# Input rows and meta tokens given by columns, with the row factor applied behind the first products

## The chip, the cores and the metric

The kernel runs on one core of one Trainium2 chip. Its five engines run side by side and wait for one another through semaphores: TensorE (PE in the profile, its weight loads PEld), VectorE (DVE), ScalarE (ACT), GpSimd (POOL) and SyncE (SP), which here only issues transfers. The metric is the device time of one execution in microseconds; lower is better. The kernel before takes 978.37 us, the median of three runs that lie between 978.27 and 979.35 us.

## The reference

Two transformer blocks are computed one after the other on 256 rows of width 1024. Only the start of the first block matters here. Sixteen meta tokens are put before the 256 input rows (272 rows together), and each row is normalised and projected:

```python
u = rms_norm(h, pre_mix_gain[l])          # each row times rsqrt(mean(row^2) + 1e-6), each column times a gain
proj = u @ w_in[l]
qa, ka, va, qb, kb, vb, g = jnp.split(proj, SPLITS, axis=-1)
qa = rope(qa...); ka = rope(ka...); qb = rope(qb...); kb = rope(kb...)
o_swa = windowed_gqa_sink_attention(qa, ka, va, attn_sink[l], pos, is_real)
o_diff = differential_attention(qb, kb, vb, lam, lambda_init, diff_subln_gain[l], is_key)
gates = jax.nn.sigmoid(g + b_gate[l])
```

`rope` multiplies by cosines and sines of the position and adds the two halves of a head; the rest of the block (two attentions, gates, output projection, feed-forward) and the whole second block follow. All of it is float32. The norm is a factor of the row times a gain of the column. A factor of the row can be applied before the product with `w_in` or behind it.

## The kernel before

**Products.** A float32 product is made of three products in a reduced format. Each weight tile is split on ACT into a rounded part `whi` (line 1968) and on DVE into the rest `wlo = raw - whi` (line 1338); the activations are split the same way into `R1[0]` and `R1[1]`. PE then adds whi x R1[0], whi x R1[1] and wlo x R1[0] (lines 796 to 798, and 920 to 922 for the first unit).

**Units and halves.** Weights come in units of 1 MB (1024 x 256 columns, 128x8x256 in a tile), four buffers `raw` deep, issued by SP at line 2515; buffer i is used again once the unit four before is split (the wait at line 2514). A unit is worked in two halves, 24 products each. A function, `schedule()`, writes one list of steps, and each engine runs in this order the steps that it knows. "ahead" steps put the splits up to four halves ahead of PE, as far as the two buffers `whi`, `wlo` allow. An engine works its own list strictly in order, so a wait holds everything behind it on that engine.

**The opening.** SP loads the input rows X, ACT issues meta tokens, the identity and the gains. ACT and DVE square the 272 rows, POOL takes the power -0.5 (line 2356), ACT and DVE scale the rows (`rows`), PE turns them to columns (`turn` and `turnm`, line 782), and ACT and DVE split them with the gain into R1 (lines 2002 and 1389). While nothing is there, PE multiplies a constant 13 times (`keep`, line 787).

**The first units.** They are: unit 0 (two blocks of `qa`), unit 1 (`ka0`), unit 2 (`va`), unit 3 (more `qa`). For each block of a query or key, ACT copies the PSUM bank with halves swapped in four pieces (line 2019, `rope` or `roped`), DVE multiplies by the cosine and sine tables (lines 1421 and 1422), POOL adds (line 2368). `swap` copies the two key blocks with their halves exchanged into KS (lines 2027 and 2028). The values go through `VT` (line 2034), a turn on PE and a copy on DVE (lines 1428 to 1435). `setup` makes small constants of the parameters; its exponential on ACT (line 2011) waits for two dot products on DVE.

**The first head.** The scores of the first head (line 941) stand on PE after the first half of unit 3. They need all of `qa` block 0, both key blocks (`rope_pool ("ka0", 1)`) and both copies of `swap` (`swap_act`). What stands behind them on PE waits too, the second half of unit 3 first. `gate(u)` is the gate's product with a tanh straight from PSUM (line 2093).

## Time and profile before

| | |
|---|---|
| median of three runs | 978.37 us |
| the profiled execution, its own time | 978.03 us |
| its span, first to last instruction | 976.2 us |
| PE busy | 949.0 us (97%) |
| DVE busy | 685.8 us (70%) |
| ACT busy | 533.3 us (55%) |
| mean granted TensorE clock | 0.995 |

The profiled execution is 0.34 us under the median, and 1.8 us of it lie outside the span. A row of the timeline gives start, duration, engine, line, operation, output<-inputs, count, and in brackets the idle time ahead of it and what ended it. Line 1962 is the helper through which all of ACT's work goes, 1338 the low split of weights, 1331 a scalar multiply on DVE. A granted clock of 1.00 is 2.4 GHz, 0.50 is 1.2 GHz. PE's matmuls overlap, so their durations do not add up; what counts is the distance from start to start.

### The profile page before, as it was taken

The page shows a single profiled execution, that of the slowest core. Times are in us where ns is not written, and L with a number is a line of the kernel's source. Part 1 is how long each engine was busy: PE and PEld are TensorE (multiplying, and loading weights), DVE is VectorE, ACT ScalarE, POOL GpSimd, SP SyncE. Part 2 cuts the span into 40 slices and gives each one's busy share as a digit, 9 for nine tenths or more (in the row PEclk, how much of TensorE's full clock was granted, in tenths as well). Part 3 has the DMA queues.
Part 4 walks back from the last instruction along what each step waited for, and adds up shares of the span by engine and source line. Part 5 has one row for each costly group of instructions (what it writes and reads, how often), then busy time and mean ns, then how long its engine had stood idle before and what let it go on. Part 6 is the DMA issues. An engine that isn't in the chain of part 4 may idle for free.

```text
span 976.2 us, 15556 instructions
## 1 busy us (share of the span) xinstructions
PE 949.0 (97%) x6212; PEld 846.6 (87%) x6212; DVE 685.8 (70%) x1251; ACT 533.3 (55%) x1019; POOL 126.4 (13%) x145
## 2 busy tenths in 40 slices
PE   8999999999999999999999999799899999999997
PEld 7999888999999988888988898698699898888885
DVE  6888776777478676766667679776665577676765
ACT  7876666765456643434355877444444364434443
POOL 2211111211032000000001139610100000000001
PEclk9999999999999999999999999999999999999999
DMA  9543334334377556565647642201353446656541
GB/s 319 188 135 131 130 112 148 99 120 134 126 260 236 174 174 215 173 216 173 204 141 247 224 165 88 87 1 44 131 172 130 151 132 210 199 170 200 171 169 43
DMA packets 115863, 154.71 MB, mean 158 GB/s; under 512 B 2728, under 2 KB 98224, under 8 KB 115536
## 3 DMA queue, kind: packets, MB, share of 16 engines
q1 hardware_dynamic: 113376, 142.91, 44.4%
q0 software_dynamic: 1952, 10.42, 3.0%
q8 instruction: 49, 0.80, 0.4%
q10 hardware_dynamic: 464, 0.40, 0.2%
q14 instruction: 22, 0.18, 0.1%
HBM read 150.56 MB, written 3.16 MB: 157 GB/s over the span
## 4 chain that ended last, share of the span: by engine, by line
PE 84%; DVE 8%; ACT 5%; issue 2%; DMA 0%; POOL 0%; POOLq 0%; DVEq 0%; ACTq 0%
PE ps L820 14%; PE ps L796 8%; PE ps L798 8%; PE ps L797 8%; PE ps L821 7%; PE ps L1107 4%; PE ps L1080 4%; PE ps L1081 4%; PE ps L1082 4%; PE ps L839 3%; PE ps L841 3%; PE ps L840 3%; PE ps L782 3%; DVE wlo L1338 2%; PE ps L809 2%; PE ps L811 2%
## 5 line engine op out<-in xcount | busy, mean ns | idle before, releaser
L1338 DVE TENSOR_TENSOR wlo<-raw,whi 128x1024 fp32r<-128x1024 f32 (+1 forms) x268 | 326.8, 1237 | 161.2 <-ACT whi L1962 160.9
L1962 ACT ACTIVATE whi<-raw 128x1024 fp32r<-128x1024 f32 (+1 forms) x268 | 274.2, 1051 | 132.8 <-PE ps L821 53.8
L820 PE MATMUL ps<-R1b,whi 128*128 128x512 f32 x576 | 201.8, 393 | 0.0
L796 PE MATMUL ps<-R1b,whi 128*128 128x256 f32 (+1 forms) x592 | 172.6, 291 | 0.8 <-DVE wlo L1338 0.8
L798 PE MATMUL ps<-R1b,wlo 128*128 128x256 f32 (+1 forms) x592 | 167.7, 283 | 0.0
L797 PE MATMUL ps<-R1b,whi 128*128 128x256 f32 (+1 forms) x592 | 167.6, 283 | 0.0
L821 PE MATMUL ps<-R1b,wlo 128*128 128x256 f32 x576 | 161.4, 280 | 0.0
L820 PEld LDWEIGHTS ps<-R1b,whi 128*128 128x128 f32 x576 | 108.1, 188 | 24.7 <-issue 0.5
L796 PEld LDWEIGHTS ps<-R1b,whi 128*128 128x128 f32 x592 | 111.5, 188 | 10.1 <-issue 7.9
L798 PEld LDWEIGHTS ps<-R1b,wlo 128*128 128x128 f32 x592 | 111.8, 189 | 0.0
L797 PEld LDWEIGHTS ps<-R1b,whi 128*128 128x128 f32 x592 | 111.5, 188 | 0.2
L821 PEld LDWEIGHTS ps<-R1b,wlo 128*128 128x128 f32 x576 | 108.2, 188 | 0.6
L2356 POOL TENSOR_TENSOR st<-st 128x1 f32<-128x1 f32 (+5 forms) x28 | 23.1, 832 | 382.4 <-DVE st L1331 299.8
L1080 PE MATMUL ps<-whi,R3ah 128*128 128x512 f32 x176 | 69.0, 392 | 1.1 <-DVE wlo L1338 1.1
L1081 PE MATMUL ps<-wlo,R3ah 128*128 128x512 f32 x176 | 68.8, 391 | 0.0
L1082 PE MATMUL ps<-whi,R3al 128*128 128x512 f32 x176 | 68.5, 389 | 0.0
L1962 ACT ACTIVATE F<-F 128x512 f32<-128x512 f32 (+6 forms) x58 | 29.3, 506 | 55.3 <-DVE F L1591 53.7
L1962 ACT ACTIVATE R3ah<-F 128x512 fp32r<-128x512 f32 x22 | 13.9, 632 | 67.8 <-DVE F L1613 67.8
L1580 DVE TENSOR_REDUCE F<-ps 128x256 f32<-128x512 f32 x72 | 49.3, 685 | 0.0
L1962 ACT ACTIVATE SC<-ps 128x512 f32<-128x512 f32 (+3 forms) x78 | 33.1, 429 | 22.8 <-PE ps L798 10.4
L1080 PEld LDWEIGHTS ps<-whi,R3ah 128*128 128x128 f32 x176 | 33.0, 188 | 9.1 <-issue 1.9
L1082 PEld LDWEIGHTS ps<-whi,R3al 128*128 128x128 f32 x176 | 33.0, 188 | 7.2
(294 smaller groups left out, 1801.3 us busy)
## 6 DMA issues: line engine op xcount, KB each, us to landing
raw<-in_w_in SPq DMA_DIRECT2D x34, 1024.0 KB, 5.0
raw<-in_w_ffn_in SPq DMA_DIRECT2D x22, 1024.0 KB, 5.1
raw<-in_w_ffn_out SPq DMA_DIRECT2D x11, 1024.0 KB, 5.5
raw<-in_w_gate SPq DMA_DIRECT2D x11, 1024.0 KB, 5.4
raw<-in_w_up SPq DMA_DIRECT2D x11, 1024.0 KB, 5.3
raw<-in_w_down SPq DMA_DIRECT2D x11, 1024.0 KB, 5.6
raw<-in_w_out SPq DMA_DIRECT2D x8, 1024.0 KB, 5.1
raw<-in_w_xkv SPq DMA_DIRECT2D x8, 1024.0 KB, 5.4
```

What stands on the lines that cost most here:

```text
L796: e.matmul(o, hi[:, kt, c], R[0][:, kt, 0:n], start=kt == 0, stop=False)
L797: e.matmul(o, hi[:, kt, c], R[1][:, kt, 0:n], start=False, stop=False)
L798: m = e.matmul(o, lo[:, kt, c], R[0][:, kt, 0:n], start=False, stop=kt == 7)
L820: e.matmul(B[:, :].rearrange("p (a n) -> p a n", a=2), hi[:, kt, c], R[2][:, :, kt, 0:256], start=kt == 0, stop=False)
L821: m = e.matmul(B[:, 0:256], lo[:, kt, c], R[0][:, kt, 0:256], start=False, stop=kt == 7)
L1080: e.matmul(B[:, :], Fh[:, k, c], hi[:, k, d], start=j == 0 and k == 0, stop=False)
L1081: e.matmul(B[:, :], Fh[:, k, c], lo[:, k, d], start=False, stop=False)
L1082: m = e.matmul(B[:, :], Fl[:, k, c], hi[:, k, d], start=False, stop=end and k == 1)
L1107: return e.matmul(o, a, b, start=True, stop=True)
L1338: e.tensor_tensor(half_of(wlo[i % HL], i, k), half_of(raw[i % RAW], i, k), f32(half_of(whi[i % HL], i, k)), SUB).then_inc(lo_split(i, (i, k)))
L1580: e.tensor_reduce(FSLOT[j % 2][0][:, at:at + 256], B[:, :].rearrange("p (a n) -> p n a", a=2), AX, ADD).then_inc(ffn_dve((kind, f, j, b)))
L1962: return e.activation(o, i, f, **kw)
```

## The change

The host now also gives the input rows and the meta tokens by columns (`x_cols`: 8 gains and 8 x 272 columns on 128 partitions, 1092 KB). They come in two halves, the first unit of weights in two halves too. R1 is split straight from them (`xsplit`), without the row factor, so that the norm's statistics and the turns on PE are no longer ahead of the first products. The row factor is applied behind the products: PE spreads it over the partitions (`rowtab`), DVE multiplies it into the cosine and sine tables and keeps a copy for the gates; values get it in the copy behind their turn; a gate's product is multiplied by it on DVE, and tanh reads that (`tanh`). The rows as such, for the statistics and for the residual, come behind unit 2, all on SP. The first unit's products go pass by pass (`ropek`). The first four blocks of `rope` take their PSUM bank from the pool "head". `swap` stands one half later, behind `setup`, `rowtab` and four rope blocks.

```diff
     def opening():
+        def laid(k, key, b):
+            step("roped", key, b, k)
+            step("rotate", key, b, k)
         order.append(("w_in", "featk", 0, 256))
         for j in range(2):
             take(0, j)
             step("ropek", j, 0)
...
+        order.append(("w_in", "feat", 1024, 256))
+        for j in range(2):
+            take(1, j)
+            step("ropep", "ka0", j, j, 1, 2 + j)
+            if j == 0:
+                step("rowstat")
+            yield 1
+        state["rope"] = 4
+        for j, _ in enumerate(values("va", 1280, 0, ("setup",))):
+            if j == 0:
+                step("rowtab")
+                laid(0, "qa", 0)
+                laid(1, "qa", 1)
+            else:
+                laid(2, "ka0", 0)
+                laid(3, "ka0", 1)
+                step("swap")
+            yield 1
...
     def gates(u):
-        return unit(("gate", u), "w_in", "feat", 4608 + 256 * u)
+        yield from unit(("gate", u), "w_in", "feat", 4608 + 256 * u)
+        step("tanh", u)
...
-    step("rows", "n1")
+    step("xsplit", 0, 4)
     ahead(1)
-    step("turn", "n1", (0, 2))
-    ahead(2)
-    step("turn", "n1", (4, 6))
-    step("turnm")
+    step("xsplit", 4, 8)
...
+            def rowtab():                                   # PE
+                B = claim("head", ("row0",), (norm_dve, "tables"))
+                p.wait_ge(id_in, 0)
+                p.wait_ge(norm_pool, "row0")
+                for i in range(2):
+                    mm(B[:, 128 * i:128 * i + 128], rs0[:, i:i + 1].to_broadcast([128, 128]), ident)
...
-                B = claim("gemm", ("rope", k), (rope_act, k), (rope_dve, ("cos", k)))
+                B = claim("head" if k < 4 else "gemm", ("rope", k), (rope_act, k), (rope_dve, ("cos", k)))
...
+                p.wait_ge(hi_split, (i, part))
+                for w, r in ((hi, 0), (hi, 1), (lo, 0)):
+                    if w is lo:
+                        p.wait_ge(lo_split, (i, part))
...
+            def xsplit(first, end):                         # DVE
+                for kt in range(first, end):
+                    d.wait_ge(norm_act, ("n1", "hi", kt))
+                    stt(R1[1][:, kt, :], xT[:, kt, :], xcols[:, kt:kt + 1], f32(R1[0][:, kt, :]), MUL, SUB)...
+            def rowtab():                                   # DVE
+                B = ps("row0")
+                d.wait_ge(norm_pe, "row0")
+                d.wait_ge(ca_in, 0)
+                for name in ("cos", "sin"):
+                    e.tensor_tensor(caf(name), caf(name), B[:, 0:NT], MUL).then_inc(norm_dve("tables"))
+                d.wait_ge(set_act, "lam")
+                e.tensor_copy(rsb0, B[:, 0:256]).then_inc(norm_dve("tables"))
...
+            def gate(u, j, i):                              # DVE
+                if j:
+                    d.wait_ge(gemm, ("gate", u))
+                    d.wait_ge(norm_dve, "tables")
+                    e.tensor_tensor(GA[:, 2 * u:2 * u + 2, :], ps("gate", u)..., rep(rsb0, 2), MUL).then_inc(gate_dve(u))
...
+            def xsplit(first, end):                         # ACT
+                a.wait_ge(xb_in if first else xa_in, 0)
+                for kt in range(first, end):
+                    act(R1[0][:, kt, :], xT[:, kt, :], scale=xcols[:, kt:kt + 1]).then_inc(norm_act(("n1", "hi", kt)))
+            def rowstat():                                  # ACT
+                for signal_, v_, m, i in ((x_in, X[:, 0, :], 128, 0), (meta_in, metat, 16, 2)):
+                    a.wait_ge(signal_, 0)
+                    act(sq0[i][0:m], v_, ACT.Square, accum_out=row0[0:m, i:i + 1]).then_inc(norm_act("sq0"))
```

On SP, which issues nearly all transfers, this is the order before, from the first one on:

```order
L2509 DMA X<-in_x 128x1024
L2510 DMA X<-in_x 128x1024
L2515 DMA raw<-in_w_in 128x8x256
L2517 DMA ca<-in_const_a 128x544
L2515 DMA raw<-in_w_in 128x8x256
L2519 DMA pc<-in_params 128x391
L2520 DMA ca<-in_const_a 128x544
```

and now (`F<-in_x_cols` are the columns, the two `128x4x256` the halves of unit 0, `ca` 128x128 the identity, the first `ca` 128x544 the cosine and sine tables, the second the masks):

```order
L2563 DMA F<-in_x_cols 128x1096
L2568 DMA raw<-in_w_in 128x4x256
L2569 DMA F<-in_x_cols 128x1088
L2570 DMA raw<-in_w_in 128x4x256
L2574 DMA raw<-in_w_in 128x8x256 x2
L2576 DMA X<-in_x 128x1024
L2577 DMA X<-in_x 128x1024
L2578 DMA F<-in_meta_tokens 16x1024
L2579 DMA ca<-in_const_a 128x128
L2580 DMA ca<-in_const_a 128x544
L2581 DMA pc<-in_params 128x399
```

Behind both lists come the further units: before, units 2 and 3 with nothing between them; now unit 3, the masks and unit 4. The rows X have moved from the front to behind unit 2, and what ACT issued is now on SP ahead of unit 3.

On ACT, from the split of units 1 and 2 to the exponential of `setup` (`whi` is a split, SE, SC and SD with 32 partitions are rope copies, SD 128x272 is a value block, F<-F 64x272 is `swap`, st<-st 128x2 the exponential), before:

```order
L1962 ACTIVATE whi<-raw 128x8x128 x3
L1962 ACTIVATE SE<-ps 32x256 x4
L1962 ACTIVATE SC<-ps 32x256 x4
L1962 ACTIVATE whi<-raw 128x8x128
L1962 ACTIVATE SD<-ps 32x272 x4
L1962 ACTIVATE whi<-raw 128x8x128
L1962 ACTIVATE SE<-ps 32x272 x4
L1962 ACTIVATE whi<-raw 128x8x128
L1962 ACTIVATE SD<-ps 128x272
L1962 ACTIVATE F<-F 64x272 x4
L1962 ACTIVATE st<-st 128x2
```

and now, from the squares of the rows (`F,st<-`) to `swap`:

```order
L2009 ACTIVATE F,st<-X 128x1024
L2009 ACTIVATE F,st<-F 16x1024
L2009 ACTIVATE whi<-raw 128x8x128 x2
L2009 ACTIVATE SD<-ps 128x272
L2009 ACTIVATE st<-st 128x2
L2009 ACTIVATE SE<-ps 32x256 x4
L2009 ACTIVATE SC<-ps 32x256 x4
L2009 ACTIVATE whi<-raw 128x8x128
L2009 ACTIVATE SD<-ps 128x272
L2009 ACTIVATE SD<-ps 32x272 x4
L2009 ACTIVATE SE<-ps 32x272 x4
L2009 ACTIVATE F<-F 64x272 x4
```

The two splits ahead of the value block are now those of unit 3, the exponential stands ahead of all four rope blocks, and these are worked in one go between unit 3's splits and `swap`. PE's own list is the same from the first scores to the end (5180 rows in either); ahead of them it has 18 rows fewer.

## Rows read from the trace of the kernel before

**Rows 1.** The page: the span, and PE's busy time.

```profile
span 976.2 us, 15556 instructions
PE 949.0 (97%) x6212; PEld 846.6 (87%) x6212; DVE 685.8 (70%) x1251; ACT 533.3 (55%) x1019; POOL 126.4 (13%) x145
```

**Rows 2.** Windows: length; PE, PEld, DVE, ACT, POOL busy (count); clock; DMA share; GB/s.

```profile
3.75:22.50 18.75, 16.31 (x118) 14.84 (x117) 13.58 (x26) 14.01 (x27) 2.79 (x4) 1.00 1.09 357
60.00:80.00 20.00, 20.00 (x165) 18.17 (x165) 16.64 (x48) 15.45 (x38) 2.88 (x4) 1.00 0.49 158
...
618.70:621.20 2.50, 2.50 (x11) 2.50 (x12) 2.50 (x4) 0.39 (x1) 2.39 (x3) 0.50 0.00 0
```

**Rows 3.** Waits of PE from 30 to 260 us: total, times, longest.

```profile
PE ps L941 <- ACT SC L1962: 2.0, 4, 0.6
```

**Rows 4.** Timeline of PE, opening to the first scores.

```profile
0.93 7.34 PE L787 MATMUL ps<-st 128*128 128x256 f32 x26 [0.93 <-DVE st L1950]
...
12.69 0.36 PE L920 MATMUL ps<-R1b,whi 128*128 128x256 f32 x1 [0.85 <-DVE R1b L1328]
...
19.31 0.36 PE L796 MATMUL ps<-R1b,whi 128*128 128x272 f32 x1 [0.77 <-DVE wlo L1338]
...
34.67 0.49 PE L782 MATMUL ps<-ca,SD 128*128 128x128 f32 x3
35.09 1.56 PE L941 MATMUL ps<-F 64*128 64x272 f32 x8
```

**Rows 5.** Timeline of SP: the issue of unit 3.

```profile
7.87 2.92 SPq L2515 DMA_DIRECT2D raw<-in_w_in  x1
```

**Rows 6.** Time from issue to landing: the first half of X, then unit 3.

```profile
X<-in_x SPq DMA_DIRECT2D x1, 512.0 KB, 4.2
...
DMA to landing us min/median/max: 12.6/12.6/12.6
```

**Rows 7.** Timeline of ACT, the first square to the exponential of `setup`.

```profile
4.91 1.06 ACT L1962 ACTIVATE F<-X 128x1024 f32<-128x1024 f32 x1 [1.50 <-DMA X<-in_x]
...
17.81 1.99 ACT L1962 ACTIVATE whi<-raw 128x1024 fp32r<-128x1024 f32 x2
19.83 1.58 ACT L1962 ACTIVATE SE<-ps 32x256 f32<-32x256 f32 x4
...
26.86 1.63 ACT L1962 ACTIVATE SE<-ps 32x272 f32<-32x272 f32 x4
28.51 1.06 ACT L1962 ACTIVATE whi<-raw 128x1024 fp32r<-128x1024 f32 x1
29.60 0.40 ACT L1962 ACTIVATE SD<-ps 128x272 f32<-128x272 f32 x1
30.20 1.79 ACT L1962 ACTIVATE F<-F 64x272 f32<-64x272 f32 x4 [0.20 <-POOL F L2368]
32.01 0.20 ACT L1962 ACTIVATE st<-st 128x2 f32<-128x2 f32 x1
```

**Rows 8.** Timeline of DVE: low splits, a sine product, the start of `setup`, a 512 copy.

```profile
17.94 3.50 DVE L1338 TENSOR_TENSOR wlo<-raw,whi 128x1024 fp32r<-128x1024 f32 x3 [0.66 <-ACT whi L1962]
...
28.88 0.43 DVE L1422 TENSOR_TENSOR SE<-SE,ca 128x272 f32<-128x272 f32 x1
...
31.17 0.16 DVE L1331 TENSOR_SCALAR st<-pc 128x16 f32<-128x16 f32 x1
...
51.95 0.68 DVE L1468 COPY SC<-ps 128x512 f32<-128x512 f32 x1
```

**Rows 9.** Timeline of POOL: the three powers, and the sum of the second key block.

```profile
6.39 2.63 POOL L2356 TENSOR_TENSOR st<-st 128x1 f32<-128x1 f32 x3 [4.58 <-DVE st L1331]
...
29.39 0.77 POOL L2368 TENSOR_TENSOR F<-SE 128x272 f32<-128x272 f32 x1 [1.97 <-DVE SE L1422]
```

**Rows 10.** Timeline of PE late in the program, where it had stood idle.

```profile
618.70 3.45 PE L1107 MATMUL ps<-SC 128*128 128x128 f32 x16 [2.62 <-DVE SC L1718]
...
634.03 2.59 PE L1107 MATMUL ps<-SC 128*128 128x128 f32 x16 [2.31 <-DVE SC L1718]
```

More of the change, by code:

```diff
@@ L340, in opening, with values @@
             step("ropek", j, 0)
-            if j:
-                for b in range(2):
-                    step("roped", "qa", b, b)
-                    step("rotate", "qa", b, b)
-                state["rope"] = 2
-            yield 1
-    def values(key, col0, u):
+            yield 1
+        order.append(("w_in", "feat", 1024, 256))
[16 more added lines that the diff above has]
+            yield 1
+    def values(key, col0, u, *then):
         order.append(("w_in", "feat", col0 + 256 * u, 256))
@@ L356, in values @@
                 step("vt", key, u, 0)
+            else:
+                for s in then:
+                    step(*s)
             yield 1
@@ L383, in schedule @@
     kb = [behind(kb[u], ("vt", "vb", u, 1)) for u in range(4)]
-    va = behind(values("va", 1280, 0), ("swap",), ("setup",))
-    units = [opening(), rope("ka0", 1024, 0), va, qa[1], ga[0], qa[2], ga[1], qa[3], ga[2], qb[0], vb[0], kb[0],
+    units = [opening(), qa[1], ga[0], qa[2], ga[1], qa[3], ga[2], qb[0], vb[0], kb[0],
              ga[3], qb[1], vb[1], kb[1], ga[4], qb[2], vb[2], kb[2], ga[5], qb[3], vb[3], kb[3], ga[6], *bs, ga[7]]
@@ L391, in schedule @@
                   [[]] * 5 + [[("merge", u)] for u in range(3)])
-    n = len(units) * 2
+    n = 2 * len(units) + 4
     at += [(n - 6, 1, ("between",))]
@@ L2085, in diff, with tanh @@
                     act(R3b[0][:, h, :], ps("O", x)[:, 256:512], scale=subg).then_inc(head_act(("oh", x)))
-            def gate(u, j, i):
-                if j:
-                    a.wait_ge(pc_in, 0)
-                    a.wait_ge(gemm, ("gate", u))
-                    a.wait_ge(set_dve, "hb")
-                    for k in range(2):
-                        act(GA[:, 2 * u + k, :], ps("gate", u)[:, 256 * k:256 * k + 256], ACT.Tanh,
-                            bias=hb[:, 2 * u + k:2 * u + k + 1], scale=0.5).then_inc(gate_act(u))
+            def tanh(u):
+                a.wait_ge(gate_dve, u)
+                a.wait_ge(set_dve, "hb")
+                for k in range(2):
+                    act(GA[:, 2 * u + k, :], GA[:, 2 * u + k, :], ACT.Tanh, bias=hb[:, 2 * u + k:2 * u + k + 1],
+                        scale=0.5).then_inc(gate_act(u))
             def merge(u):
```

134 lines of the change are left out of this document (72 added, 62 removed).

## The prediction

> **What bounds the kernel now.** I read the page first: PE is busy for 949.0 of 976.2 us [rows 1], so only what moves PE's work in time, or makes it wait, can count. Windows come next. From 60 to 80 us PE is busy for all 20.00 us with 165 products, 0.121 us from one to the next, while DVE has 16.64 and ACT 15.45 us of work [rows 2]; the waits say the same: from 30 to 260 us PE waits for another engine 4 times, 2.0 us in all, each time for exponentials ahead of scores [rows 3]. The reader is to see that behind the opening PE runs at its own rate, and that what is lost or won ahead of that stretch arrives at the end unchanged. Then PE's timeline: constant products until 8.27, first real product at 12.69, the second unit at 19.31, and from there without a gap to the first scores at 35.09 [rows 4]. So the start costs time, and the change goes for it. PE's list is the same from the first scores to the end, so one number decides: when these scores start, 35.09 us now. The last view is therefore of what the scores need: transfers, ACT, DVE and POOL up to there [rows 5 to 9].
>
> **The opening (removed: statistics, scaling and turns ahead of the products).** The first half of the columns is about as large as the first half of X, which landed 4.2 us after its issue and was being read at 4.91 [rows 6, 7]. Four column splits at 0.40 (the 128x272 copy) and a weight split of 1.0 [rows 7] put the first product at some 7.6 us in place of 12.69, where the 12 constant products end too. The second unit is bound by its transfer. Measured, the queue is never slack: 357 GB/s from 3.75 to 22.50 us [rows 2]. Unit 3 landed at 7.87 + 12.6 = 20.5 us [rows 5, 6] as the last of 5992 KB (X 1024, meta 64, units 0 to 3 4096, identity 64, tables 272, parameters 200, masks 272). Now 6812 KB come up to it (columns 1092, X, meta, identity, tables, parameters 204, four units; the masks come behind). That is 820 KB or 0.84 MB more, 2.35 us at 357 GB/s: **unit 3 lands at 22.8 us**. Unit 1 lands 3672 KB before it, 10.5 us earlier, at 12.3; with a split of 1.0 and a low split of 3.50/3 = 1.17 [rows 7, 8] PE starts it at 14.5 in place of 19.31. That is the gain, 4.8 us, if it survives.
>
> **What is late next.** The scores wait for `swap`, `swap` for the second key block's sum, and now all four rope copies stand on ACT behind unit 3's two splits and behind the exponential. Nothing of this could start earlier. X and the meta tokens land 1560 KB ahead of unit 3, at 18.3, their second square (1.06 plus some 0.2 for its sum [rows 7]) ends at 19.6, and ACT then stands before unit 3's split with nothing else to do, 3.2 us. The steps, each at its measured length:
> - 22.8, two splits, 1.99 [rows 7]: 24.9 with the start's delay of 0.1. The second low split on DVE behind them, 1.17 after the first, which ends at 25.1 [rows 8]: 26.3.
> - `setup` starts behind these low splits; from its first instruction at 31.17 to the exponential at 32.01 it took 0.84 [rows 7, 8]. Exponential at 27.1, ACT free of it by 27.2.
> - Two rope copies of 1.60 each with their gap: 30.4. A split of unit 4, 1.08: 31.5. The value copy, 0.42: 31.9. Two key copies of 1.65 each: 35.2 [rows 7].
> - From the end of the last key copy (26.86 + 1.63 = 28.49) DVE's cosine and sine products, POOL's sum (29.39, 0.77) and `swap` took until 30.20 + 1.79 = 31.99, 3.50 us [rows 7 to 9]: **38.7**.
>
> The scores start at 38.7 in place of 35.09: **+3.6 us**, and the 4.8 us won are idle time of PE ahead of them. The row factor itself is in time: POOL's three powers took 2.63 [rows 9], one now covers all three columns, so it is ready by 21; DVE's tables follow the exponential at 28.3, ahead of the second rope copy's end. One smaller wait shows: PE's first value turn takes the bank that these tables free, about 28.3 against the 26.5 at which PE is there (five halves and a turn took 34.67 + 0.33 - 19.31 = 15.7, 3.0 us a half [rows 4]). It is covered by the larger one behind it. Bounds of this term: if unit 3 landed as early as before, the chain would start with the value block at 23.5 and end at 35.5, +0.4; with DVE and POOL getting in each other's way on every step as badly as the rows allow, one more us, +4.6. I take 3.6, since each item has its own row.
>
> **The clock.** PE is through with the first half of unit 3 and the second value turn at about 32.4, so it stands idle for 6.3 us ahead of the scores. Idle stretches of 2.62 and 2.31 us stand late in the program [rows 10], and behind the first one the granted clock is 0.50 for 2.5 us of work, which is 1.2 GHz, half the work at the same time: 1.25 us lost in that window [rows 2]. The new stretch is over twice as long and ahead of dense products. I take 1.5 us, between 0 (the early waits near 0.8 us [rows 4] cost nothing) and 2.5. The Trainium skill, "TensorE: Matmul & The Clock Gate", section on HAM oscillation, says that a wait between groups of matmuls sends the array back to its low clock and that the next group starts cold. This trace agrees (0.50 behind the 2.62 us of idle); by that rule the sum is the one below, without it 1.5 us less.
>
> **The other edits.** Eight gate products get a DVE multiply of 512 columns from PSUM, priced by the 512 copy at 0.68 us [rows 8]: 5.4 us more on DVE between 45 and 250 us. They lie beside PE's work, in DVE's free 3.36 of 20 us [rows 2], and tanh reads SBUF instead of PSUM at about the same length. If such a multiply falls ahead of a maximum that scores wait for, one of the four waits [rows 3] grows by up to 0.68: between 0 and 2.7 us. I take 0.3, since the four waits have only 2.0 us together and the multiply is off that chain in most places. The value copies become multiplies of the same size, the memset and the three small matmuls of `rowtab` (the turn of similar size took 0.49 [rows 4]) lie in time that PE waits anyway, and the first unit pass by pass has the same 48 products. The transfers moved from ACT to SP add no bytes and are counted above. Unit 4 lands 1296 KB (itself and the masks) behind unit 3, 3.7 us later at 26.5, long before PE asks for it.
>
> **Sum.** 3.6 + 1.5 + 0.3 = 5.4 us. The profiled execution's own time is 978.03 with a span of 976.2 and 1.8 us around it; 983.4 on its scale, 0.34 more on that of the median: **983.8 us**.
>
> **The rivals.**
> - *S, the late transfer is not late.* If the first transfers moved faster than the 357 GB/s of the rows, unit 3's split would be bound by PE (the first buffers come free with unit 1's second half at 20.5) and the chain by the value block at 23.5. The scores then start at 35.5, +0.4, and with the idle stretch of 4 us the clock may add 0 to 1.5: 978.8 to 980.5, taken as 979.6. For it: large rows of 4 KB in the columns. Against it: a share of 1.09 with all 16 engines busy already [rows 2]. The Trainium skill, "DMA: Bandwidth & Descriptors", section "Anatomy of one DMA", gives about 2.0 us plus bytes over 436 GB/s for a transfer issued on POOL; the 6.98 MB would then be in at 0.7 + 2.0 + 16.0 = 18.7 us, an estimate from that page. The trace does not agree, with 357 GB/s.
> - *C, the stall without the clock.* As forecast, but the clock stays at 1.00: 982.3. For it: 1.50 us and less of idle early on cost nothing. Against: both late stretches.
> - *G, the gates tip DVE.* DVE has 83% in the window of 60 to 80 us [rows 2]; if seven multiplies each delay a low split or a maximum that PE is about to need, 7 x 0.68 = 4.8 us come on top: 988.6. Against: low splits run up to four halves ahead.
> - *F, the opening's gain arrives.* If `swap` were through when PE comes to the scores, PE would start them at 14.5 + 5 x 3.0 + 2 turns of 0.5 = 30.5, 4.6 us ahead: 973.8. It decides for this if the exponential is over by 18.9 us, since ACT and its followers need 11.6 us from there. Against it stand unit 3's landing and its two splits in ACT's own list ahead of it.
>
> **How the numbers follow.** Forecast 62%, C 16%, S 10%, G 6%, F 4%, and 2% that the change does nothing that can be seen (978.4). A measurement of this kernel tells some 0.2%, 2.0 us, from no change. Slower by more: the forecast, C, G and a third of S, 0.87; within: two thirds of S and the rest, 0.09; faster: F, 0.04. The range takes in the forecast with a us off in the chain and the clock between its bounds, C and the upper part of S: 980.2 to 986.8.
>
> **What would show it.** In the profile after: first product near 7.6 and unit 1 near 14.5; ACT idle for about 3 us ahead of unit 3's first split, which starts near 22.9; exponential near 27.1; the first scores at 38.7 with an idle stretch ahead of them that ends with ACT's F<-F copies; a clock near 0.50 right there; PE busy all through 60 to 80 us. I am wrong if the scores start before 35 us, if unit 3's split starts before 21, or if PE has new waits behind 60 us of over 1 us in sum.

## The result, and the profile after

The changed kernel takes 988.74 us (median; 986.42 to 989.21), the kernel before beside it 978.32 us (978.05 to 979.35): a ratio of 1.0108, 95% interval [1.0095, 1.0121]. It is slower, as forecast, but by 10.4 us in place of 5.4, and outside the range of 980.2 to 986.8.

The page of the changed kernel (span, then busy time of each engine), to be held against [rows 1]:

```profile
span 984.6 us, 15518 instructions
PE 950.3 (97%) x6192; PEld 847.2 (86%) x6192; DVE 689.2 (70%) x1255; ACT 533.2 (54%) x1016; POOL 125.6 (13%) x143
```

PE has 1.3 us more busy time; the rest of the 8.4 us of span is idle. Of the four timed runs the profiled one is the fastest (986.42), so the span tells less than the median. A mark in the program tells more: the first product of 512 columns in the first feed-forward (FFN) starts at 339.7 us in place of 329.6, 10.1 us late, which agrees with the medians. These are the groups of that product, in the kernel before and in the changed one (shortest, median and longest in ns, then first and last start):

```profile
L820 PE MATMUL ps<-R1b,whi x576: 387/393/470, 329.6 to 940.5; 128*128 128x512 f32 x192
```

```profile
L843 PE MATMUL ps<-R1b,whi x576: 387/393/470, 339.7 to 948.9; 128*128 128x512 f32 x192
```

Behind the mark the two profiled executions differ by 1.7 us the other way (648.4 and 646.7 us of device time). Runs of one kernel fall into groups 1 to 2 us apart (the kernel before, beside later runs: 976.3 to 977.1 and 977.8 to 978.7 us), so a median can come from either, and a difference of less than 2 us is better read at the mark. All ledgers below stop at that mark.

The opening first. PE's timeline (start, duration, tile, shape, count, and what ended the idle time before), against [rows 4]:

```profile
8.88 2.25 PE L945 MATMUL ps<-R1b,whi 128*128 128x256 f32 x16
...
29.75 0.55 PE L805 MATMUL ps<-ca,SD 128*128 128x128 f32 x3 [1.73 <-DVE pc L1435]
...
40.66 2.19 PE L964 MATMUL ps<-F 64*128 64x272 f32 x8 [7.07 <-issue]
```

The first product starts 3.8 us sooner (8.88 against 12.69), and PE is at the first value turn (L805) at 28.0 us, where it waits until 29.75; in the kernel before the same turn starts at 31.50. All that is won there is idle time ahead of the scores at 40.66. The first product itself waited for no data: the first weights were split at 7.2 us (ACT 6.19 + 1.04), but PE multiplied constants until 8.9. What the scores waited for is on ACT (against [rows 7]):

```profile
18.09 1.06 ACT L2009 ACTIVATE F<-F 16x1024 f32<-16x1024 f32 x1
...
23.91 2.01 ACT L2009 ACTIVATE whi<-raw 128x1024 fp32r<-128x1024 f32 x2 [4.67 <-DMA raw<-in_w_in]
25.82 0.38 ACT L2009 ACTIVATE SD<-ps 128x272 f32<-128x272 f32 x1
28.02 0.21 ACT L2009 ACTIVATE st<-st 128x2 f32<-128x2 f32 x1 [1.82 <-DVE st L1357]
28.25 1.57 ACT L2009 ACTIVATE SE<-ps 32x256 f32<-32x256 f32 x4
...
34.60 1.62 ACT L2009 ACTIVATE SE<-ps 32x272 f32<-32x272 f32 x4
38.63 1.78 ACT L2009 ACTIVATE F<-F 64x272 f32<-64x272 f32 x4 [2.41 <-POOL F L2421]
```

It is the chain of the forecast, link by link, and each link later than forecast: unit 3's splits at 23.9 (22.9), exponential 28.0 (27.1), end of the last key copy 36.2 (35.2), end of `swap` 40.4 (38.7). From the splits to the last key copy it took 12.3 us, as forecast; only the landing and the last step are longer. The last step took 4.2 us in place of 3.5: DVE began it 0.3 us behind the key copy, being still at the block before, and then met POOL (against [rows 8, 9]):

```profile
36.90 0.87 DVE L1459 TENSOR_TENSOR SE<-SE,ca 128x272 f32<-128x272 f32 x1
```

```profile
36.71 0.76 POOL L2421 TENSOR_TENSOR F<-SD 128x272 f32<-128x272 f32 x1 [3.69 <-DVE SD L1459]
```

The sine product, begun 0.19 us behind POOL's sum, takes 0.87 us, against 0.43 without one; POOL's sum has its usual 0.76.

The windows (length; PE, PEld, DVE, ACT, POOL busy; clock; DMA share; GB/s), against [rows 2]:

```profile
0.75:24.00 23.25, 23.07 (x146) 21.60 (x147) 11.98 (x20) 12.98 (x20) 1.92 (x3) 1.00 1.02 339
...
42.00:44.00 2.00, 2.00 (x9) 1.30 (x8) 1.94 (x5) 1.93 (x4) 0.00 (x0) 0.50 0.12 27
...
60.00:80.00 20.00, 19.64 (x155) 16.92 (x154) 15.23 (x36) 14.89 (x36) 2.42 (x4) 1.00 0.45 148
```

Transfers ran at 339 GB/s on the mean of a window that holds their start; from 3.75 to 22.50 us, the stretch of [rows 2], it is 362 GB/s against 357, so they were no slower. Behind the 7.07 us of idle the clock is 0.50 (1.2 GHz); and between 60 and 80 us PE, which had not one idle stretch there before, has 0.36 us of it. That last line is the part of the loss that the forecast did not have. The waits of PE from 30 to 260 us (total, times, longest), against [rows 3]:

```profile
PE ps L964 <- issue: 7.1, 1, 7.1
PE ps L964 <- ACT SC L2009: 3.4, 4, 1.4
PE ps L805 <- DVE pc L1435: 1.7, 1, 1.7
PE ps L994 <- DVE SC L1509: 1.0, 2, 0.7
```

What PE waited 2.0 us for on ACT ahead of scores it now waits 3.4 us for, and a wait for DVE's copy ahead of the probabilities' turn (L994) is new. One of its two places, in DVE's rows and then in PE's; the gate's multiply (L1560) stands right ahead of the copies:

```profile
71.69 0.68 DVE L1560 TENSOR_TENSOR SE<-ps,pc 128x512 f32<-128x512 f32 x1
72.29 0.68 DVE L1507 COPY SC<-ps 128x512 f32<-128x512 f32 x1
72.89 0.28 DVE L1509 COPY SC<-ps 128x128 f32<-128x128 f32 x1
```

```profile
73.22 0.71 PE L994 MATMUL ps<-SC,SD 128*128 128x128 f32 x4 [0.36 <-DVE SC L1509]
```

So the ledger to the mark is: first scores +5.6 (35.09 to 40.66); from there to the second scores +1.25 (10.21 to 11.46, the clock); from there to the mark +3.3 (284.3 to 287.6), of which 2.4 us are these waits and the other 0.8 to 0.9 us do not show as idle.

### The profile page after: what moved, and what is told of

It is laid out like the page before. It is cut to its first block, busy times and chain, and to the rows that moved or that the text cites. A ratio compares the mean times of both kernels' runs of the same rounds, so it can differ in the third digit from the quotient of the medians.

```text
span 984.6 us, 15518 instructions
## 1 busy us (share of the span) xinstructions
PE 950.3 (97%) x6192; PEld 847.2 (86%) x6192; DVE 689.2 (70%) x1255; ACT 533.2 (54%) x1016; POOL 125.6 (13%) x143
## 4 chain that ended last, share of the span: by engine, by line
PE 76%; DVE 11%; ACT 8%; issue 2%; DMA 1%; SPq 1%; POOL 0%; POOLq 0%; DVEq 0%; ACTq 0%
PE ps L843 14%; PE ps L844 7%; PE ps L819 6%; PE ps L821 6%; PE ps L820 6%; PE ps L1130 4%; PE ps L1103 4%; PE ps L1104 4%; PE ps L1105 4%; PE ps L862 3%; PE ps L864 3%; PE ps L863 3%; DVE wlo L1361 3%; ACT whi L2009 3%; PE ps L805 2%
## 5 line engine op out<-in xcount | busy, mean ns | idle before, releaser
L843 PEld LDWEIGHTS ps<-R1b,whi 128*128 128x128 f32 x576 | 108.1, 188 | 24.7 <-issue 0.5
L2405 POOL TENSOR_TENSOR st<-st 128x2 f32<-128x2 f32 (+5 forms) x26 | 21.4, 825 | 396.7 <-DVE st L1354 313.9
```

The costliest lines, as they stand in the source:

```text
L843: e.matmul(B[:, :].rearrange("p (a n) -> p a n", a=2), hi[:, kt, c], R[2][:, :, kt, 0:256], start=kt == 0, stop=False)
```

## The experiments

The table gives for every kernel the start of the first and second scores, the mark, and the last distance, all of the profiled execution; then the median and the ratio to the kernel before as it ran beside that kernel (its medians there were 977.8 to 978.3 us). The diffs are cut: `...` stands for what is left out. In the rows with * the heads stand later in PE's list, so that more products precede the scores, and only the mark compares.

| kernel | first | second | mark | second to mark | median us | ratio [95%] |
|---|---|---|---|---|---|---|
| before | 35.09 | 45.30 | 329.6 | 284.3 | 978.32 | |
| after | 40.66 | 52.12 | 339.7 | 287.6 | 988.74 | 1.0108 [1.0095, 1.0121] |
| gates_alone | 35.05 | 45.28 | 333.8 | 288.5 | 980.71 | 1.0034 [1.0023, 1.0044] |
| gates_psum | 40.34 | 52.08 | 336.5 | 284.4 | 985.12 | 1.0077 [1.0050, 1.0103] |
| gates_behind | 40.48 | 52.94 | 344.0 | 291.1 | 991.30 | 1.0145 [1.0130, 1.0160] |
| gates_short | 40.95 | 53.68 | 338.7 | 285.0 | 987.06 | 1.0098 [1.0084, 1.0111] |
| gates_pool | 40.89 | 53.26 | 337.7 | 284.4 | 985.34 | 1.0079 [1.0067, 1.0091] |
| warm_gap | 41.30 | 51.14 | 339.7 | 288.6 | 987.60 | 1.0099 [1.0076, 1.0122] |
| copies_first | 38.42 | 49.67 | 337.5 | 287.8 | 986.62 | 1.0089 [1.0072, 1.0106] |
| copies_gates | 38.53 | 50.91 | 341.9 | 291.0 | 988.79 | 1.0120 [1.0105, 1.0135] |
| rotates_first | 37.42 | 49.92 | 337.3 | 287.4 | 985.29 | 1.0074 [1.0061, 1.0086] |
| best | 37.41 | 47.25 | 333.4 | 286.2 | 981.76 | 1.0041 [1.0027, 1.0056] |
| tables_first | 36.38 | 46.30 | 332.5 | 286.2 | 981.67 | 1.0036 [1.0023, 1.0049] |
| scores_later * | 40.23 | 52.37 | 337.4 | | 985.77 | 1.0080 [1.0055, 1.0104] |
| all_early_7 * | 42.54 | 52.37 | 339.4 | | 986.03 | 1.0092 [1.0077, 1.0107] |
| tables_first_7 * | 37.68 | 47.51 | 330.4 | | 978.95 | 1.0008 [0.9999, 1.0017] |
| one_ahead_7 * | 36.46 | 46.39 | 330.5 | | 979.04 | 1.0008 [0.9998, 1.0018] |
| one_ahead_7b * | 36.63 | 48.05 | 330.6 | | 977.64 | 1.0005 [0.9996, 1.0015] |

**gates_alone**: the kernel before, with nothing but the multiply on DVE (by a row of ones) and the hyperbolic tangent behind it, one step later.

```diff
+        step("tanh", u)
...
+                    e.tensor_tensor(GA[:, 2 * u:2 * u + 2, :], ps("gate", u)[:, :]..., rep(par("lam", 0, 256), 2), MUL).then_inc(gate_dve(u))
...
-                    a.wait_ge(gemm, ("gate", u))
+                a.wait_ge(gate_dve, u)
```

> The kernel before, with one part of the change alone: each gate product goes through a DVE multiply (here by ones) into SBUF, and tanh reads that. In the traces PE's lead over the same place of before grew from 6.8 us of delay at the second scores to 10.0 us at those near 186 us, with the opening long over. Theory G: these 3.2 us are the eight multiplies on DVE and the later tanh, so this kernel takes 978.3 + 3.2 = 981.5 (980.8 to 982.2) and shows new waits of PE for DVE and longer ones for the exponentials. Rival: the multiplies are hidden as priced in the prediction (0.3) and the 3.2 us are an after-effect of the late first head: 978.3 to 979.

The mark moves by 4.2 us, without any change of the opening. PE's waits from 30 to 260 us:

```profile
PE ps L942 <- ACT SC L1971: 3.4, 4, 1.4
PE ps L972 <- DVE SC L1472: 1.9, 3, 0.9
```

These are the two waits of the changed kernel. The gates cost some us by themselves. That is theory G, though with 4.2 us at the mark for its 3.2. The median, 980.71, moves by only 2.7 us, but the shortest times (980.51 against 976.33) lie 4.2 us apart, as the mark does.

**gates_psum**: the changed kernel with the tangent reading the bank, as before; the row factor is left out of the gates.

```diff
-        step("tanh", u)
...
-                    e.tensor_tensor(GA[...], ps("gate", u)..., rep(rsb0, 2), MUL).then_inc(gate_dve(u))
```

> The changed kernel with the gates as in the kernel before: tanh reads the product from PSUM, and the row factor is left out of the gates. Theory G: 988.7 - 3.2 = 985.5, with the first scores still near 40.7 us. Rival (after-effect of the late head): 988.4.

Everything behind the second scores is as in the kernel before: 284.4 us, and the same wait as [rows 3]:

```profile
PE ps L963 <- ACT SC L2001: 2.0, 4, 0.6
```

What is left, 6.9 us at the mark, is the opening and the clock. That is theory G again, 985.12 for 985.5.

**gates_behind**: the changed kernel, multiply one step later, just ahead of the tangent.

```diff
+        step("gmul", u)
         step("tanh", u)
```

> The changed kernel with the gate multiply on DVE one step later in the order (with tanh), so that DVE does not stand waiting for the gate's product with other work behind it. Theory P (place): the 3.2 us that gates cost come from DVE waiting in its order for the product; they go to under 1, time 985.5 to 986.5. Rival L (length): the eight multiplies of 0.68 us themselves hold up the exponentials and turns of the heads; the cost stays at 2.5 us or more, time 988 to 989.

Theory P is refuted, and the time is above rival L's 988 to 989 too: the kernel lost 3.5 us more behind the second scores, with multiplies of the same length, so their place counts as well. ACT now waits in other places, and a value turn waits for it:

```profile
PE ps L965 <- ACT SC L2009: 3.4, 4, 1.3
PE ps L995 <- DVE SC L1510: 2.0, 2, 1.1
PE ps L806 <- ACT SC L2009: 1.5, 1, 1.5
```

**gates_short**: is it DVE's time, or ACT's wait behind DVE's queue? The multiply is cut to 16 of 256 columns; the tangent reads the bank itself, so the row factor is left out of the gates and the bank comes free only behind the tangent.

```diff
-                    e.tensor_tensor(GA[:, 2 * u:2 * u + 2, :], ps("gate", u)[:, :]..., rep(rsb0, 2),
+                    e.tensor_tensor(GA[:, 2 * u:2 * u + 2, 0:16], ps("gate", u)[:, :]...[:, :, 0:16], rep(rsb0, 2)[:, :, 0:16],
```

> The changed kernel with each of the eight gate multiplies of VectorE cut to 16 of its 256 columns; the hyperbolic tangent reads the products' bank itself, still behind the multiply. So the row factor is left out of 240 of 256 tokens' gates (and of the rest too, since the tangent reads the bank); every wait between TensorE, VectorE and ScalarE stays. Theory L (length): what the gates cost is VectorE's time, eight times 0.68 us in a stretch in which it is nearly always needed; with some 0.15 us each the kernel goes to the time of the version whose gates never touch VectorE, 985.1 us, with the first FFN product at 336.5 to 337.2 us. Theory W (chain): what they cost is that the tangent waits for VectorE's queue, and through it ScalarE and the bank; then the time stays at 988 to 989 us and the first FFN product at 339.0 to 340 us. Between them, each has its share.

One multiply took 0.18 us in place of 0.68, and 2.6 of the 3.3 us are gone (285.0). The waiting of ACT is hardly less, as its row in front of a tangent shows, first in the changed kernel, then here:

```profile
122.94 0.91 ACT L2009 ACTIVATE SE<-SE,st 128x256 f32<-128x256 f32 x2 [3.39 <-DVE SE L1560]
123.76 1.04 ACT L2009 ACTIVATE whi<-raw 128x1024 fp32r<-128x1024 f32 x1
124.82 1.57 ACT L2009 ACTIVATE SD<-ps 32x256 f32<-32x256 f32 x4
126.42 0.60 ACT L2009 ACTIVATE SC<-ps 128x512 f32<-128x512 f32 x1
```

```profile
122.59 0.84 ACT L2009 ACTIVATE SE<-ps,st 128x256 f32<-128x256 f32 x2 [2.89 <-DVE SE L1560]
...
125.99 0.60 ACT L2009 ACTIVATE SC<-ps 128x512 f32<-128x512 f32 x1
```

Both wait some 3 us. The copy of the turned probabilities out of their bank (128x512) ends at 127.0 in the one, and PE's next scores start then; half a us, the multiply's own length, is what PE feels (1.35 us of waiting for ACT at 127.07 in the changed kernel, 0.78 here, 0.64 in the kernel before). So theory L holds in the main, and the wait by itself, at this place in the order, is worth at most 0.7 us. The median, 987.06, is nearer to theory W's, but that comes from the head: the clock fell twice here (0.73 from 31 to 36 us, 0.50 from 42 to 46), and the second scores came 1.6 us later than in gates_psum, 0.6 us of it already at the first scores.

**gates_pool**: ACT copies the bank (128x512), POOL multiplies in SBUF, the tangent one gate later.

```diff
-                    e.tensor_tensor(GA[...], ps("gate", u)..., rep(rsb0, 2), MUL).then_inc(gate_dve(u))
+                    act(GA[:, 2 * u:2 * u + 2, :], ps("gate", u)[:, :]...).then_inc(gate_cp(u))
+                    pool.wait_ge(gate_cp, u)
+                    e.tensor_tensor(GA[...], GA[...], rep(rsb0, 2), MUL).then_inc(gate_pool(u))
+            step("tanh", u - 1)
```

> The changed kernel with the gate multiply taken to POOL, the whole computation kept: ScalarE copies the products of both halves out of the bank in one instruction (128x512), POOL multiplies them by the row factors in SBUF, and the tangent comes one gate later. Theory L: VectorE loses 8 x 0.68 us; ScalarE gains eight copies of about 0.6 to 0.7 us in a stretch where it is under two thirds busy, so the time comes to 985 to 986.5 us and the first FFN product to 336.5 to 338 us. Rival R: POOL's multiply of 512 columns (over 1.2 us each by its sum of 272 columns in 0.76 us) slows the VectorE instructions beside it, as its last sum made a 0.43-us product take 0.87, and the eight copies stand ahead of score exponentials on ScalarE; then nothing is won: 988 to 991 us, first FFN product at 339 us or later.

284.4 us again: with the whole computation kept, the gates cost nothing. That is theory L's forecast (985.34 us, mark 337.7). One POOL multiply, and the DVE instruction beside it:

```profile
71.11 1.31 POOL L2428 TENSOR_TENSOR SE<-SE,pc 128x512 f32<-128x512 f32 x1 [2.39 <-ACT SE L2005]
```

```profile
71.60 0.84 DVE L1357 TENSOR_SCALAR st<-st 128x2 f32<-128x2 f32 x1
```

Rival R's mechanism is there: that DVE instruction takes 0.17 us elsewhere, and five of the eight multiplies held one up, by 0.14 to 0.67 us. But nothing of it reached PE, nor did the copies of 0.6 us on ACT, so as a price of time R falls.

**warm_gap**: 18 constant products in PE's idle stretch.

```diff
+                    if x == 0:
+                        keep(ps("va", 0, 1), 18, half..., half...)
```

> The changed kernel with 18 constant products (some 0.34 us each at the full clock, 6.1 us) on PE ahead of the first scores, where it otherwise stands idle for 7 us. The scores' start stays near 40.7 since it hangs on ACT's copies. Theory K (the clock): no stretch below 1.00 there, the time falls by 1.25 us of the profiled run and by up to 3.5 us of the median, whose runs were 2.3 us longer than the profiled one: 985.2 to 987, and the runs lie closer together. Rival: the spread of 2.8 us between runs has another cause, and the time is 988.7 less 1.25 with the spread as before.

They took PE 7.9 us (33.4 to 41.3), the granted clock is 1.00 from 36 to 51 us, and first to second scores is 9.84 us in place of 11.46. The low clock costs 1.6 us up to the second scores in the changed kernel. The scores themselves came 0.6 us later, and waits for DVE behind the second scores, 1.9 us up to 100 us against 1.0 in the changed kernel, gave back the rest (288.6): nothing is won at the mark. The median of 987.60 is over theory K's 985.2 to 987 and at the rival's 987.5; the four runs lie within 1.4 us in place of 2.8. The window from 36 to 40 us (against 0.68 in the changed kernel):

```profile
36.00:40.00 4.00, 4.00 (x20) 3.49 (x19) 1.72 (x4) 1.52 (x5) 1.51 (x2) 1.00 0.01 2
```

**scores_later**: the first heads later in PE's list, so that it has products in place of the gap.

```diff
-STARTS = [6, 9, 12, 15, 18, 22, 26,
+STARTS = [8, 11, 13, 16, 19, 22, 26,
```

> The changed kernel with the first head's steps two halves of a unit later (the next four heads one or two halves later or as they were), so that PE has 48 products to do while ACT works off its copies. Theory W (the wait of the first scores for swap costs 5.6 us and the clock): the wait shrinks to about 1.2 us, clock at 1.00, 988.7 - 5.6 - 1.3 to - 3 = 980 to 982, less what the heads lose by standing closer. Rival: PE's time is lost to the later chain anyway (low splits and banks that come later): 986 or more.

The mark moved by 2.3 us and the median by 3.0, to 985.77, nearly the rival's 986; theory W's 980 to 982 is out of reach. The gap went from 7.1 to 1.4 us, but a value turn then waited for DVE, which had come to the first heads' work at the same time:

```profile
PE ps L805 <- DVE SC L1354: 3.7, 1, 3.7
PE ps L964 <- ACT SC L2009: 2.4, 3, 1.4
PE ps L964 <- issue: 1.4, 1, 1.4
PE ps L819 <- DVE wlo L1361: 1.0, 1, 1.0
```

**copies_first**: ACT's first three rope copies and `setup` ahead of unit 3's splits, in the 4.67 us in which ACT stood.

```diff
+                step("roped", "qa", 0, 0)
+                step("roped", "qa", 1, 1)
+                step("roped", "ka0", 0, 2)
+                step("setup")
...
-        for j, _ in enumerate(values("va", 1280, 0, ("setup",))):
+        for j, _ in enumerate(values("va", 1280, 0)):
```

> The changed kernel with ACT's order alone altered: the copies of the first three rope blocks and setup with its exponential stand ahead of unit 3's two splits, in the 4.7 us in which ACT now waits for that unit. Theory A (the scores are late because ACT has all rope copies and the exponential behind unit 3's landing at 23.9 us): the exponential ends by 24.2, the last key copy by 31.5 to 34, the scores start at 35 to 37 in place of 40.7, and the time falls by 4 to 7 us to 982 to 985. Rival: the scores hang on the tables, banks or transfers that come later still, and stay at 40 us or more; time 988.

The exponential went from 28.0 to 24.3 us, the scores only from 40.7 to 38.4, and it stayed so to the mark (337.5). Theory A's first links hold, but neither its scores at 35 to 37 us nor its 982 to 985 us (986.62). ACT was done with its last copy at 32.1; the rest went to DVE, whose third and fourth rotation stood behind a low split and the value copies and ended at 35.6, so that `swap` came late:

```profile
36.43 1.78 ACT L2013 ACTIVATE F<-F 64x272 f32<-64x272 f32 x4 [4.29 <-POOL F L2425]
```

**copies_gates** (copies_first and gates_behind) and **all_early_7** (all four copies and the swap early, multiply behind, heads at 7 and 10) tried sums of these.

> Both edits together, copies first and the gate multiply one step later. If theories A and P hold and their effects add: scores at 35 to 37, then no growth of the delay beyond 1 us over the heads, 978.5 to 981. If only one holds, 982 to 986.

> As copies_gates, and all four rope blocks with swap behind the first value half, and the first two heads one half of a unit later (starts 7 and 10 in place of 6 and 9), so that PE has 24 more products ahead of the first scores. By theories A and W PE waits less than 1.5 us in one piece, the clock stays at 1.00, and the opening's gain of 4.8 us arrives in part: scores near 35 with one more half of a unit done than in the kernel before, so 974.5 to 978. Rival: the value copies and low splits that now come later on DVE hold PE instead: 978 to 982.

Both missed every number expected of them (988.79 against 986 at most, 986.03 against 982 at most). The first is copies_first's head with gates_behind's loss (291.0): the two are independent. In the second the fourth copy waits for its buffer pair on ACT ahead of the value copy, and PE waits for that:

```profile
PE ps L809 <- ACT SD L2012: 5.0, 1, 5.0
```

**rotates_first** (the diff is against the changed kernel, without the lines of copies_first): copies_first, with the third rotation in the first half's steps, and `late` (the fourth's copy and products, and the swap) ahead of the value copies.

```diff
-            else:
-                laid(2, "ka0", 0)
-                laid(3, "ka0", 1)
-                step("swap")
+                step("rotate", "ka0", 0, 2)
...
             if j:
+                for s in late:
+                    step(*s)
                 step("vt", key, u, 0)
```

> The version with ScalarE's three rope copies and its setup ahead of unit 3's splits, which gave 986.6 us and its first scores at 38.4 us, with two more moves: the third rotation's products stand ahead of the second low split of unit 3 on VectorE, and the fourth's copy, products and the swap ahead of the first value copy. Theory D: the scores waited there for VectorE's products of the third and fourth rotation, which stood behind the value copies to 33.6 us; they go forward by 1.5 to 2.5 us, the scores to 36.0 to 37.0 us, and the time to 984.5 to 985.2 us. Rival V: the value copies then end 2 us later, the second value turn waits for them on TensorE, and TensorE has the same work left ahead of the scores: scores at 38.0 to 38.6 us and 986.3 to 987 us.

1.0 us at the scores and 1.3 us in the median: 37.42 us lies between what theory D (36.0 to 37.0) and rival V (38.0 to 38.6) gave, and the median, 985.29, just above D's 985.2. At the mark only 0.2 us are left. DVE's rows show the next link: the tables, which tables_first below makes at 24.7 us, stand behind 2.36 us of low splits.

```profile
26.12 2.36 DVE L1364 TENSOR_TENSOR wlo<-raw,whi 128x1024 fp32r<-128x1024 f32 x2 [0.54 <-ACT whi L2012]
28.39 0.78 DVE L1436 TENSOR_TENSOR ca<-ca,ps 128x272 f32<-128x272 f32 x2
```

**best**: rotates_first, gates_pool and ten constant products.

> All that helped together, the whole computation kept: ScalarE's rope copies ahead of unit 3's splits, the third and fourth rotation ahead of the value copies, the gate multiply on POOL, and ten constant products on TensorE (128x256) ahead of the first scores in place of the 18 that kept the clock at 1.00. If the parts add: 988.7 less 2.1 for the copies, 1.7 for the rotations, 2.5 for the gates and 1.0 for the clock is 981.4 us, first scores at 36.5 to 37.2 us, the clock 1.00 from 31 to 50 us. If POOL's multiply wins nothing, 983.5 to 984.5 us; if the rotations win nothing either, 985 to 986 us. Not below the kernel before (978) in any of them: the head chain would still be 1.5 us late.

981.76 us for the 981.4 expected if the parts add. Here 284.3 us behind the second scores became 286.2, although the gates are off DVE: two waits of 1.2 us in sum for DVE's copy ahead of the probabilities' turn, since the head now hands DVE its work sooner than DVE can do it.

**tables_first**: without the constant products, and on DVE alone the tables, `rsb0` and three rotations ahead of two low splits. **tables_first_7**: the same, with the heads half a unit later (the last two lines of the diff).

```diff
+            s0 = [n for n in range(r0) if plan[n][0] == "split"][-2]
+            head = [n for n in range(s0, len(plan)) if plan[n] in [("rowtab",)] + ...]
+            ranks = [*range(s0), *head, *[n for n in range(s0, len(plan)) if n not in head]]
-STARTS = [6, 9, 12, 15, 18, 22, 26,
+STARTS = [7, 10, 13, 16, 19, 22, 26,
```

> The version called best, without the constant products, and with the rotary tables, the row factors' copy and the first three rotations put ahead of two low splits on VectorE (there they stood behind 2.36 us of them). Theory H: the head chain is now tables, rotation, ring of three pairs, fourth copy, fourth rotation, POOL's sum, swap, each waiting for the last; the tables go from 28.2 to 25.2 us, the fourth copy from 31.0 to 28.5 us, the swap ends 2 us earlier, the first scores start at 35.0 to 35.6 us (before: 35.1), nothing is left of the head's delay, and the time is 979.5 to 980.5 us. Rival B: VectorE is behind with everything at that place (two value copies, low splits, score corrections), so what the head gives is taken back by the second and third scores, as in best, where two waits of 0.7 us for VectorE's score correction came up: the first FFN product stays at 332.5 to 333.5 us and the time at 981 to 982 us.

> The same kernel with the first five attention heads one half step later in TensorE's order (7, 10, 13, 16, 19 in place of 6, 9, 12, 15, 18). Theory B: VectorE's backlog behind the head is what is left; with a half unit of products (3.1 us) more ahead of the scores it is worked off, TensorE has no idle stretch ahead of the scores and the clock stays; second scores to first FFN product falls from about 286 us to 284.3 to 285.0 us as in the version with the later heads, and the time is 978.5 to 980 us. Theory H: what is left is the head alone, and it no longer matters; then the later heads win nothing, the time is that of tables_first within 0.5 us or longer.

The first moved the scores to 36.4 and the mark by 0.9 us; the median stayed where it was: rival B. The second is the one that gives the 10 us back, to 0.8 us at the mark: no gap ahead of the scores, and PE's 60 to 80 us is full again:

```profile
PE ps L825 <- DVE wlo L1367: 1.8, 1, 1.8
PE ps L970 <- ACT SC L2012: 1.7, 3, 0.6
PE ps L1000 <- DVE SC L1515: 1.1, 1, 1.1
PE ps L811 <- DVE st L1363: 0.4, 1, 0.4
```

```profile
60.00:80.00 20.00, 20.00 (x164) 18.24 (x164) 16.77 (x48) 13.87 (x33) 3.88 (x6) 1.00 0.49 158
```

**one_ahead_7** (only the first rotation ahead of the low splits) and **one_ahead_7b** (the fourth rotation ahead of the third low split too).

> tables_first_7 with only the tables and the first rotation ahead of the two low splits on VectorE; the second and third rotation stand behind them. There TensorE waited 1.8 us for a low split (ended some 30 us) at 29.96 us. Theory H: the splits end 1.7 us earlier, the wait goes, the fourth rotation is hardly later (its copy needs only the first one's sum), and the time falls by 1 to 1.8 us: 977.2 to 978.0 us, at or just under the kernel before. Rival B: VectorE's order only moves the wait: TensorE waits later for the swap or a value copy, and the time stays at 978.5 to 979.5 us.

> The same, and the fourth rotation ahead of the third low split too, so the swap ends some 1 us earlier, and that split 0.9 us later. Theory H: with the heads at 7 TensorE has work until the scores, so an earlier swap is worth nothing: within 0.5 us of one_ahead_7. Rival B: the order at this place counts whatever it is; the time differs by 1 us or more either way.

The wait of 1.8 us for the low split went, and 2.1 us of idle ahead of the scores came: the mark stays at 330.5 and 330.6. Rival B of the first: at that place the order on DVE only says who waits. Of the second, the medians differ by 1.4 us (rival B's sign) and the marks by 0.1 us (theory H); the mark is the better witness, as said with the result. By their ratios none of the three versions can be told from the kernel before; their marks are 0.8 to 1.0 us later. One more reading: behind the same 2.09 us of idle the clock stayed at 1.00 in one_ahead_7 and was 0.50 for 2 us in one_ahead_7b. That cost 1.5 us up to the second scores (48.05 against 46.39, the first 0.17 later) and 0.1 us at the mark.

## Why the prediction was wrong

- *What bounds the kernel.* Right as far as it went: what the head loses arrives at the end. gates_psum shows it cleanly (+6.8 us at the second scores, +6.9 at the mark, 284.4 us between them).
- *The opening's gain.* Half right. The first product came at 8.9 (7.6 forecast; the constants lasted longer), unit 1 at about 14.8 (14.5). The whole gain became idle time ahead of the scores, as forecast.
- *What is late next: forecast +3.6, measured +5.6.* The mechanism was right, two of its links undersized. Unit 3 was 1.1 us late: "the masks come behind" was wrong as a count of bytes, since at 339 GB/s over the 23.2 us to its landing 7.9 MB had come in, 0.9 MB more than the 6.98 counted up to it. In the kernel before it was 0.3 MB more by 20.5 us (324 GB/s from 0.75 us). (The 204 KB of parameters in the forecast's list are 200 in its sum, which changes nothing.) The last step took 0.7 us more: 0.44 of them are the sine product beside POOL's sum, a bound in the forecast ("one more us") and not in its sum, and 0.3 DVE's late start. Then 0.25 us from the swap's end to the scores.
- *The clock: forecast 1.5, measured 1.25 against the kernel before and 1.6 against warm_gap.* Right up to the second scores. The Trainium skill, "TensorE: Matmul & The Clock Gate", section on HAM oscillation, has the next group start cold after a wait, and this trace agrees: 0.50 behind 7.07 us of idle, and 1.00 in warm_gap, where PE did not stand ahead of the scores. The price is not fixed: behind 5.7 to 7.0 us of idle first to second scores took 11.7 to 12.7 us in gates_psum, gates_behind, gates_pool and gates_short, 1.5 to 2.5 us over the kernel before, and the profiled execution of the changed kernel is its fastest. Nor does it always arrive: warm_gap won nothing and one_ahead_7b lost 0.1 us at the mark, with DVE as the next bound.
- *The gates: forecast 0.3 in a range of 0 to 2.7, measured 3.3 here and 4.2 in gates_alone.* This is the step that failed: "they lie beside PE's work, in DVE's free 3.36 of 20 us". A busy share of 83% is not 17% of room: where DVE's multiply stands ahead of what PE is about to need, it goes through to PE, in whole or in part. Two such places are direct (L994), two go over ACT: DVE's multiply, then the tangent, a split and two groups of copies in ACT's list, the last of which, and no exponential as the forecast had it, frees what the scores wait for. The forecast looked at the second chain and took it for off the path "in most places". It was on it in two of four, with 0.71 us each, its whole length. [rows 3] had been read wrongly there: in the kernel before too, these waits end with ACT's copies out of PSUM (the longest with that of the turned probabilities, 117.11 to 117.71 us, ahead of scores at 117.76) and not with exponentials. Rival G named the mechanism and put 4.8 us on it, at 6%; that its 988.6 us are the time measured is luck, since it has the gates 1.5 us too dear and the head 2.0 us too cheap.
- *The sum.* 5.6 + 1.25 + 3.3 = 10.1 against 3.6 + 1.5 + 0.3 = 5.4. Of the 4.7 us missing, 3.0 are the gates', 2.0 the head's, less 0.25 for the clock.
- *The rivals.* S fell: unit 3 was later, not sooner. C fell by the clock. F fell; and where the head's chain was shortened by 4.3 us (tables_first) no more than the loss came back: its 973.8 was not in reach, since DVE's work on the first heads is the next bound.

What stays open: the 0.8 us between second scores and mark in the changed kernel that no idle stretch shows; why the gates cost 4.2 us in gates_alone and 3.3 us here; what the later heads alone would do to the kernel before, which no run shows; and whether a version with this opening can beat the kernel before. The three that undo its costs end level with it.

## What to carry to other kernels

What this case suggests: work put on an engine that is not the bottleneck is free only where no short chain from it reaches the bottleneck engine: list the waits of the bottleneck engine, walk each back two links, and price new work at its full length wherever one of the links is in that engine's queue. Starting the first product sooner is worth nothing until every consumer's chain at the first hand-over is sooner too; here four links in turn (ACT's copies, DVE's rotations, DVE's tables, DVE's backlog) took the place of the one removed. When an elementwise step is forced by a change of algebra, look for the engine with 13% first: on POOL the same multiply took 1.3 us in place of 0.68 and, with a copy on ACT, cost PE nothing.

## What the runs showed of the hardware

- Where DVE and POOL met, the one that began later took longer: on DVE a 128x272 sine product begun 0.19 us behind POOL's sum 0.87 us in place of 0.43, and low splits begun 0.25 us behind one 1.57 us in place of 1.22 (changed kernel, at 36.90 and 32.53 us); on POOL a sum begun 0.17 us behind a low split 1.66 us in place of 0.74 (gates_pool, at 46.84 us).
- Behind 7.1, 5.8 and 4.1 us of idle of PE the granted clock was 0.50 for the first 2 us (changed kernel, copies_first, rotates_first). Behind 2.1 us (tables_first, at 30 us) it was 0.61 from 31 to 33 us, behind 2.2 us once 0.73 on the mean of 31 to 36 us (gates_short) and once 1.00 (gates_pool), behind 2.09 us once 0.50 (one_ahead_7b) and once 1.00 (one_ahead_7), behind 1.7 us 1.00 (changed kernel). Its price up to the second scores was 1.25 to 1.6 us in the changed kernel and 1.5 to 2.5 us in four relatives of it.
- From 3.75 to 22.50 us transfers ran at 357 GB/s in the kernel before and 362 in the changed one. Transfers issued behind one that is waited for took part of the rate: when unit 3 landed, 0.9 MB more had come in than was issued up to it.
